# State-space layer of a four-layer backbone: u sent through DRAM by quarters, half of the contributions moved between the gate's chunks

## The chip, the cores and the metric

The kernel runs on one core of a Trainium2 chip. The metric is the device time of one execution in microseconds (us), as the median of repeated runs.

## The reference, cut to what matters

The backbone has four layers; layer 1 is the bidirectional diagonal state-space layer (S5) that this change is about. There are 384 tokens (128 of context, 256 latent), and 2048 channels in 128 groups of 16, each group with a complex state of 64.

```
u, gate = split(h @ w_in, 2)                 # 2048 + 2048 columns
for di in (forward, backward):
    bu[t] = b_bar @ u[t]                     # per group: 16 channels -> 64 complex states
    bu[edge] += a_bar * h0
    x[t] = a_bar * x[t -+ 1] + bu[t]         # the scan; context and latent tokens each on their own,
    yd[t] = real(c @ x[t])                   # latent tokens start from a given state
y = gelu(d * u + yd_forward + yd_backward)
y = y * sigmoid(y @ w_glu + b_glu)
out = (y * silu(gate)) @ w_out
```

## The kernel before, in words

Each core engine runs one program: TensorE (PE) the matmuls, ScalarE (ACT) and VectorE (DVE) the rest, GpSimd (POOL) and SyncE (SP) issue DMAs. Weights come in chunks of 1 MiB through a ring of four buffers. After each chunk of a layer's weight comes a chunk of `ada_w`, the modulation of the next layer, which PE takes with 4 matmuls from the ring (line 331). SP loads chunks in this one order (`load_chunk`, line 261): a chunk may be loaded when the chunk four places before it has been used, so an `ada_w` chunk waits for PE's matmuls on the one two chunks earlier, and everything behind it in SP's queue waits too. ACT rounds a chunk to `w_hi` (line 399, `split_chunk`), DVE makes the rest `w_lo` (line 406), and PE takes three products of it (`group_sums`, line 302, 48 matmuls for a chunk of u, gate or glu). Two `w_hi`/`w_lo` buffers alternate. Four chunks make a group of 512 output channels.

Layer 1 runs so:

- u: 4 groups. ACT and DVE copy the sums to `s5_uT` (lines 2350, 2444).
- When all of u is there, POOL stores it to DRAM (line 2199), waits, and gathers it back into `s5_u`, where rows are 8 tokens x 16 channels: two DMAs of single elements (line 2204) and eight of runs of 48 elements (line 2208). It runs beside the gate's chunks.
- gate: 4 groups; ACT writes SiLU of the sums to `s5_gateT`. Then all engines meet (`mix1.projected`), and POOL stores the gate to DRAM (line 2213).
- Contributions: for k of 0 to 15 (8 groups each), SP loads 1 MiB of prepared weights (`wk`, line 2230; `wk[0]` has a place of its own, `spare`; the other three lie over the hT tile's words in `scratch`), PE does 64 matmuls (line 2297), ACT and DVE copy them out of PSUM to the states `hs` (lines 463 and 2402).
- Scans: with 8 steps of tokens folded into the prepared weights, 31 steps remain; DVE scans states 0 to 7 of k (`hs[0]`), then 8 to 15 (`hs[1]`), with six instructions a step (lines 2425, 2431, 2435).
- Outputs: for each k, `cak` and `tk` are loaded (1 and 0.5 MiB, lines 2240, 2243), PE multiplies states by them (lines 2321, 2327), ACT copies (line 463), PE turns the result round (line 2338), ACT takes the gelu of it (line 2396). k = 0 waits for the contributions of all 16 k and the first scan, k = 8 for the second scan.
- y is split into hi and lo by quarters (lines 456, 460) after all 16 k, then glu's chunks begin.

Of the kernel before, what the change touches and what calls it, by code (L numbers as in the profile page):

```python
# [13 lines left out]
P = 128  # L14
# [116 lines left out]
def build(nc, ins, outs, consts, layers=range(DEPTH)):  # L131
    ctx = ExitStack()
    with ctx:
# [219 lines left out]
        def ada_rows(a):  # L353

            at = [place for end, place in ((8, 6144), (21, 22240), (24, 12800), (32, 12288), (36, 19200), (48, 12928)) if a < end]
            return view(at[0], GC)

        def act_ada(a):
            nc.scalar.wait_ge(ada_used, 4 * (a + 1))
            if a == ADA_START:  # L360
                nc.scalar.wait_ge(x_saved, 16)
            act_copy(ada_rows(a), banks[4][:, :])
            nc.scalar.drain().then_inc(ada_copied, 1)
# [1786 lines left out]
        spare = view(20224, 2048)  # L2150
        wk = [spare] + [hT_words[:, n * 2048:(n + 1) * 2048] for n in range(3)]
# [27 lines left out]
        bwd_taken_late = sem("bwd_taken_late")  # L2179
        scan_multiplied = sem("scan_multiplied")  # L2180
        scan_summed = sem("scan_summed")
        scan_stepped = sem("scan_stepped")
# [9 lines left out]
        def pool_s5(pool, l):  # L2192
            pool.wait_ge(h_lo_ready, h_quarter(f"norm{l}", 3))
            nc.gpsimd.dma_start(st_rows, w["state_s5"].rearrange("a b d (g h) n r -> (a b d g) (h n r)", h=2))\
                .then_inc(h0_in, 16)
            nc.gpsimd.memset(s5_u[:, :, SCH:SCE], 0.0).then_inc(u_zero, 1)

            pool.wait_ge(u_evacuated, 2)
            nc.gpsimd.dma_start(ud_dram.rearrange("(k p) n -> p k n", p=P), s5_uT).then_inc(u_parked, 16)
            pool.wait_ge(u_parked, 16)  # L2200
            pool.wait_ge(u_zero, 1)
            for rows, col, tok in ((slice(112, 128), SCH, 0), (slice(0, 16), SCH + 1, CTX - 1)):
                at = tok % ST * SCH + tok // ST
                nc.gpsimd.dma_start(s5_u[rows, :, col:col + 1],
                                    ud_dram[:, at:at + 1].rearrange("(g p) c -> p g c", p=SC),
                                    allow_slow_non_contiguous=True).then_inc(u_in, 16)
            for j in range(ST):
                nc.gpsimd.dma_start(s5_u[16 * j:16 * j + 16, :, 0:SCH],
                                    ud_dram[:, j * SCH:(j + 1) * SCH].rearrange("(g p) c -> p g c", p=SC))\
                    .then_inc(u_in, 16)  # L2210

            pool.wait_ge(stage_done, after(f"mix{l}.projected"))
            nc.gpsimd.dma_start(gate_dram, s5_gateT.rearrange("p a b -> p (a b)")).then_inc(gate_parked, 16)
            pool.wait_ge(y_ready, 8)
            nc.gpsimd.dma_start(s5_gate_back.rearrange("p a b -> p (a b)"), gate_dram).then_inc(gate_back, 16)
            pool.wait_ge(state_copied, 1)
            nc.gpsimd.dma_start(outs[4].rearrange("a b d (g h) n r -> (a b d g) (h n r)", h=2), st_rows)\
                .then_inc(state_stored, 16)
            pool.wait_ge(state_stored, 16)

        def sp_s5(sp, l):
            sp.wait_ge(x_saved, 16 * parked(l))
            for k in range(16):
                if k == 0:
                    sp.wait_ge(s5_w_stored, 16 * HB)
                if k == 1:
                    sp.wait_ge(stage_done, after(f"mix{l}.projected"))
                if k >= 4:
                    sp.wait_ge(s_ready, k - 3)
                nc.sync.dma_start(wk[k % 4], wbt_dram[k]).then_inc(wk_in[k % 4], 16)  # L2230
            for k in range(16):
# [4 lines left out]
                if k == 3:  # L2236
                    sp.wait_ge(s_ready, 13)
# [7 lines left out]
        u_evacuated = sem("u_evacuated")  # L2245

        def pe_s5(pe, st, l):
            for name in ("u", "gate"):
                for g in range(4):
                    first = (name, g) == ("u", 0)  # L2250
                    group_sums(pe, f"{name}{l}", g, [P] * 4, bank_wait=first_banks(l) if first else None,
                               inputs=f"norm{l}" if first else None)
# [3 lines left out]
            pe.wait_ge(h0_in, 16)  # L2256
            for r in range(2):
                nc.tensor.transpose(banks[7][:, r * P:(r + 1) * P], st_rows[:, r::2], ident[:, :])
            nc.tensor.drain().then_inc(h0_turned, 1)
            pe.wait_ge(u_in, 16 * (ST + 2))  # L2260

            for k in range(16):
                pe_contributions(pe, k)
# [11 lines left out]
            nc.tensor.drain().then_inc(state_turned, 1)  # L2275
            for g in range(4):
# [3 lines left out]

        def pe_contributions(pe, k):


            pe.wait_ge(wk_in[k % 4], 16 * (k // 4 + 1))
            if k >= 2:
                pe.wait_ge(fwd_taken, k - 1)
                if k < 10:
                    pe.wait_ge(bwd_taken, k - 1)
                else:
                    pe.wait_ge(bwd_taken_late, k - 9)  # L2290
            for gi in range(4):
                for d in range(2):
                    for r in range(2):
                        at = (2 * gi + r) * SCE
                        for h in range(2):
                            w0 = (2 * gi + h) * 256 + (2 * d + r) * SN
                            mm = nc.tensor.matmul(banks[2 * (k % 2) + d][64 * h:64 * h + 64, at:at + SCE],
                                                  wk[k % 4][:, w0:w0 + SN], s5_u[:, 8 * k + 2 * gi + h, :],
                                                  start=True, stop=True, skip_group_check=True)
            mm.then_inc(s_ready, 1)  # L2300

        def pe_outputs(pe, l, k):
# [4 lines left out]
            if k == 0:  # L2307
                pe.wait_ge(fwd_taken, 16)
                pe.wait_ge(bwd_taken_late, 8)
# [33 lines left out]
        def act_s5(act, st, l):  # L2343
            def u_write(g):
                for m in range(2):
# [3 lines left out]
                    bank_free(nc.scalar, m)  # L2349
            stream("act", f"u{l}", u_write)  # L2350
            nc.scalar.drain().then_inc(u_evacuated, 1)
# [6 lines left out]
            stream("act", f"gate{l}", gate_write)  # L2358
            st.at(f"mix{l}.projected")
            act.wait_ge(u_parked, 16)  # L2360
            for k in range(16):
                act.wait_ge(s_ready, k + 1)
                if k == 8:
                    act.wait_ge(gate_parked, 16)
                take_contributions(act_copy, k, 0).then_inc(fwd_taken, 1)
                if k >= 8:
                    take_contributions(act_copy, k, 1).then_inc(bwd_taken_late, 1)
            for k in range(16):
# [11 lines left out]
            split_h("act")  # L2380
# [18 lines left out]

        def take_contributions(copy, k, d):  # L2400
# [4 lines left out]
        def dve_scan(dve, half):  # L2405
# [3 lines left out]
            bk = banks[7][:, 0:2 * P].rearrange("p (r d h g) -> p r d h g", r=2, d=2, h=2)  # L2409
            for d, (zero, first) in enumerate(((0, 16), (15, 47))):  # L2410
                v.memset(h_[:, zero, d, :, :], 0.0)
                v.tensor_copy(h_[:, first, d, :, :], bk[:, :, d, half, :])
            v.drain()
            for s in range(31):
# [6 lines left out]
                for d in range(2):  # L2421
                    if s:
                        dve.wait_ge(scan_stepped, 2 * (31 * half + s - 1) + d + 1)
# [3 lines left out]
                                    .broadcast_to([P, 2, segs, 64]), ALU.mult).then_inc(scan_multiplied, 1)  # L2427
                for d in range(2):
                    dve.wait_ge(scan_multiplied, 2 * (31 * half + s) + d + 1)
                    t = [scan_t[:, d, w, 0:segs, :].rearrange("p s (r g) -> p s r g", r=2) for w in range(2)]  # L2430
                    v.tensor_tensor(t[0], t[0], t[1][:, :, ::-1, :], ALU.add).then_inc(scan_summed, 1)
                for d in range(2):
                    dve.wait_ge(scan_summed, 2 * (31 * half + s) + d + 1)
                    n_ = h_[:, nxt[d], d, :, :].rearrange("p s r g -> p s (r g)")
                    v.tensor_tensor(n_, n_, scan_t[:, d, 0, 0:segs, :], ALU.add).then_inc(scan_stepped, 1)
            v.drain().then_inc(scanned, 1)

        def dve_s5(dve, st, l):
            v = nc.vector

            def u_write(g):
                for m in range(2, 4):
# [3 lines left out]
                    bank_free(v, m)  # L2446
            stream("dve", f"u{l}", u_write)
            v.drain().then_inc(u_evacuated, 1)
            stream("dve", f"gate{l}")
            st.at(f"mix{l}.projected")  # L2450

            dve.wait_ge(u_parked, 16)
            for k in range(8):
                dve.wait_ge(s_ready, k + 1)
                take_contributions(v.tensor_copy, k, 1).then_inc(bwd_taken, 1)
            dve.wait_ge(h0_turned, 1)
            dve.wait_ge(fwd_taken, 8)
            dve.wait_ge(bwd_taken, 8)
            dve_scan(dve, 0)
            dve.wait_ge(fwd_taken, 16)  # L2460
            dve.wait_ge(bwd_taken_late, 8)
            dve_scan(dve, 1)
# [8 lines left out]
            split_h("dve")  # L2471
# [67 lines left out]
        def sp_program(sp):  # L2539
# [3 lines left out]
            for l in layers:  # L2543
# [12 lines left out]
                if l % 3 == 1:  # L2556
                    load_job(sp, f"u{l}", 4, w["s5_w_in"][j], 0)
                    load_job(sp, f"gate{l}", 4, w["s5_w_in"][j], D)
# [49 lines left out]
```

## Time and profile before

| what | value |
|---|---|
| median of 3 runs | 3464.74 us (3463.69 to 3467.09) |
| the profiled execution's own time | 3458.35 us |
| its span in the profile | 3456.6 us |
| PE busy | 3179.6 us (92%) |
| DVE busy, ACT busy | 1462.8 us (42%), 1062.3 us (31%) |
| chain that ended last, by engine | PE 67%, DVE 8%, DMA 7%, PEld 7% |
| mean granted clock of TensorE | 0.966 of full |

The span runs from the first to the last instruction. Busy time is the time in which an engine had an instruction under way. PEld is PE's loading of weights, which overlaps its matmuls. The chain that ended last is followed back from the last instruction, at each step to what released it. The granted clock is 1.0 at 2.4 GHz and 0.5 at 1.2 GHz.

### The profile page before, as it was taken

Reading aid. Unit: us, or ns where it says so; the run is one execution under the profiler, and the core shown is the slowest. Engines: PE = TensorE matmul, PEld = TensorE weight load, DVE = VectorE, ACT = ScalarE, POOL = GpSimd, SP = SyncE. Lnnn points to the kernel's source line nnn. Section 1 sums busy time; section 2 is a strip of 40 time slices with the busy share of each in tenths; the row PEclk is TensorE's granted clock in tenths of the full one; section 3 lists DMA queues with packets and bytes.
Section 4 is the critical chain, followed back from the end, with each engine's and each line's share of the span. In section 5 each row is a group of like instructions: output and inputs, shape, how many; then the busy total and the mean of one; then the engine's idle time right before and its main releaser. Section 6 shows DMA issues by size and latency. Waiting matters only on the chain.

```text
span 3456.6 us, 47210 instructions
## 1 busy us (share of the span) xinstructions
PE 3179.6 (92%) x20134; PEld 2659.4 (77%) x20134; DVE 1462.8 (42%) x2137; ACT 1062.3 (31%) x1433; POOL 185.5 (5%) x285
## 2 busy tenths in 40 slices
PE   5699899989899997879999899999999999999988
PEld 2488788866677986767988677886877998986777
DVE  3499852344434221192243454323334332244443
ACT  1333333222324212123232343323333323322322
POOL 1033330000000000000000000000000000000000
PEclk7899999999999998899999999999999999999999
DMA  9899985511364687785652555565443443421132
GB/s 357 312 334 353 316 295 210 199 57 37 110 214 165 219 219 196 271 321 216 219 192 79 178 200 190 183 215 195 163 167 118 132 125 121 136 88 37 37 124 96
DMA packets 288096, 639.18 MB, mean 185 GB/s; under 512 B 21280, under 2 KB 54192, under 8 KB 277264
## 3 DMA queue, kind: packets, MB, share of 16 engines
q1 hardware_dynamic: 262896, 524.58, 44.0%
q0 software_dynamic: 24992, 111.59, 9.4%
q8 instruction: 159, 2.61, 0.3%
q14 instruction: 49, 0.40, 0.0%
HBM read 561.01 MB, written 75.04 MB: 184 GB/s over the span
## 4 chain that ended last, share of the span: by engine, by line
PE 67%; DVE 8%; DMA 7%; PEld 7%; issue 4%; ACT 3%; PEldq 2%; DVEq 1%; ACTq 0%; POOL 0%; SPq 0%; POOLq 0%
PE bank L302 35%; PE bank L306 21%; PE bank L331 4%; DMA raw<-in_ada_w 3%; PEld bank L770 2%; DMA raw<-in_s_w_in 2%; PEld bank L764 2%; DVE arena L1996 1%; DVE w_lo L406 1%; DMA raw<-in_mla_w_in 1%; DVE arena L2425 1%; DMA s_in_dram<-arena 1%; PEld bank L820 1%; PE bank L609 1%; ACT hT_hi L456 1%
## 5 line engine op out<-in xcount | busy, mean ns | idle before, releaser
L406 DVE TENSOR_TENSOR w_lo<-raw,w_hi 128x2048 fp32r<-128x2048 f32 (+3 forms) x364 | 619.0, 1717 | 1216.3 <-ACTq L400 1212.5
L302 PE MATMUL bank<-hT_hi,w_hi 128*128 128x384 f32 (+1 forms) x2608 | 904.1, 347 | 56.9 <-DVEq L407 35.7
L399 ACT ACTIVATE w_hi<-raw 128x2048 fp32r<-128x2048 f32 (+3 forms) x364 | 521.5, 1452 | 1300.8 <-PE bank L302 670.6
L302 PE MATMUL bank<-hT_lo,w_hi 128*128 128x384 f32 (+1 forms) x2608 | 887.4, 340 | 0.0
L302 PE MATMUL bank<-hT_hi,w_lo 128*128 128x384 f32 (+1 forms) x2608 | 886.8, 340 | 0.0
L302 PEld LDWEIGHTS bank<-hT_hi,w_hi 128*128 128x128 f32 (+1 forms) x2608 | 493.7, 189 | 129.1 <-issue 82.2
L302 PEld LDWEIGHTS bank<-hT_lo,w_hi 128*128 128x128 f32 (+1 forms) x2608 | 493.9, 189 | 1.5
L302 PEld LDWEIGHTS bank<-hT_hi,w_lo 128*128 128x128 f32 (+1 forms) x2608 | 493.2, 189 | 1.4
L306 PE MATMUL bank<-w_hi,hT_hi 128*128 128x512 f32 x1056 | 424.7, 402 | 12.5 <-DVE hT_lo L460 12.2
L306 PE MATMUL bank<-w_lo,hT_hi 128*128 128x512 f32 x1056 | 419.5, 397 | 0.0
L306 PE MATMUL bank<-w_hi,hT_lo 128*128 128x512 f32 x1056 | 419.4, 397 | 0.0
L463 ACT ACTIVATE arena<-bank 128x512 f32<-128x512 f32 (+5 forms) x298 | 157.4, 543 | 383.2 <-PE bank L331 114.2
L306 PEld LDWEIGHTS bank<-w_hi,hT_hi 128*128 128x128 f32 x1056 | 200.9, 190 | 79.9 <-issue 35.2
L331 PE MATMUL bank<-raw,silu_pad 128*32 128x512 f32 x1536 | 213.9, 633 | 51.5 <-DMA raw<-in_ada_w 45.7
L306 PEld LDWEIGHTS bank<-w_hi,hT_lo 128*128 128x128 f32 x1056 | 200.7, 190 | 47.5
L306 PEld LDWEIGHTS bank<-w_lo,hT_hi 128*128 128x128 f32 x1056 | 200.9, 190 | 44.8
L1996 DVE TENSOR_TENSOR arena<-arena 128x896 f32<-128x896 f32 (+1 forms) x128 | 142.3, 1153 | 6.0 <-issue 4.5
L942 ACT ACTIVATE arena<-bank,small 128x384 f32<-128x384 f32 (+1 forms) x96 | 47.8, 507 | 255.1 <-DVEq L1104 255.1
L331 PEld LDWEIGHTS bank<-raw,silu_pad 128*32 128x32 f32 x1536 | 32.0, 110 | 113.7 <-DMA raw<-in_ada_w 66.4
L770 PE MATMUL bank<-w_hi,hT_hi 128*128 128x256 f32 x512 | 99.5, 288 | 5.5 <-DVEq L748 1.8
L764 PE MATMUL bank<-hT_hi,w_hi 128*128 128x512 f32 x256 | 85.3, 415 | 14.2 <-DVE hT_hi L1087 6.6
L770 PEld LDWEIGHTS bank<-w_hi,hT_hi 128*128 128x128 f32 x512 | 80.8, 188 | 18.6 <-issue 14.0
(324 smaller groups left out, 2739.8 us busy)
## 6 DMA issues: line engine op xcount, KB each, us to landing
raw<-in_ada_w SPq DMA_DIRECT2D x192, 1024.0 KB, 5.3
raw<-in_mla_w_in SPq DMA_DIRECT2D x64, 768.0 KB, 7.4
raw<-in_gla_w_in SPq DMA_DIRECT2D x48, 1024.0 KB, 7.5
raw<-in_mla_w_in SPq DMA_DIRECT2D x40, 1024.0 KB, 7.0
raw<-in_mla_w_out SPq DMA_DIRECT2D x32, 1024.0 KB, 5.3
raw<-in_s_w_in SPq DMA_DIRECT2D x32, 1024.0 KB, 7.5
s_out_dram<-arena POOLq DMA_DIRECT2D x32, 512.0 KB, 5.8
s_in_dram<-arena POOLq DMA_DIRECT2D x16, 1024.0 KB, 9.1
```

The costliest lines, as they stand in the source:

```text
L302: mm = nc.tensor.matmul(banks[m][0:width, 0:TOK], wp[:, slot, k, at:at + width], hp[:, kt, :], start=(first and n == 0), stop=(last and n ...
L306: mm = nc.tensor.matmul(banks[m][:, 0:cols], hp[:, kt, m * P:(m + 1) * P], wp[:, slot, k, 0:cols], start=(first and n == 0), stop=(last an ...
L331: mm = nc.tensor.matmul(banks[4][32 * k:32 * k + 32, :], silu_pad[:, at:at + 32], raw_of("ada", a, s)[:, k, :], start=(s == 0), stop=(s == ...
L399: nc.scalar.activation(dst, src_, ACT.Copy)
L406: nc.vector.tensor_tensor(dst, src_, pick(w_hi, *part)[0], ALU.subtract)
L456: nc.scalar.activation(hT_hi[:, k, :], h32[:, k, :], ACT.Copy)
L463: return nc.scalar.activation(out, in_, ACT.Copy)
L609: mm = nc.tensor.matmul(banks[6 + c][:, (k % 4) * P:(k % 4 + 1) * P], G_small[:, k, c:c + 1].broadcast_to([P, P]), ident[:, :], start=True ...
L764: mm = nc.tensor.matmul(banks[7][:, 0:KEYS], wp[:, slot, kt, j * 256:j * 256 + P], cp[:, kt, :], start=(kt == 0 and m == 0), stop=(kt == 3 ...
L770: mm = nc.tensor.matmul(banks[7][:, (t % 2) * 256:(t % 2 + 1) * 256], cp[:, kt, t * P:(t + 1) * P], wp[:, slot, kt, :].rearrange("p (h x) ...
L942: nc.scalar.activation(p_sb[:, h % 2, t, 0:b - a], score_bank(h, t), ACT.Exp, scale=SM_SCALE, bias=mx[:, t:t + 1], accum_out=sm[:, t:t + 1])
L1996: nc.vector.tensor_tensor(to, powers, f, ALU.mult)
```

## The change

In u's part, each group of u is stored to DRAM and gathered back into `s5_u` as soon as it is copied out, so there are four stores and 40 gathers in place of one and 10, of a quarter's size each. The gate is stored by quarters too.

The contributions of k = 0 to 7 move into the gate's groups: after gate chunk n (n of 1 to 8) PE does the 64 matmuls of k = n - 1, in two halves into banks 6 and 7; ACT takes half 0 and DVE half 1 two chunks later in their streams. SP loads `wbt_dram[k]` in two halves into `spare` for it, between the gate's chunks, after PE has read the halves before. DVE begins the first scan after gate chunk 11 of its stream: four steps after each of 6 chunks, the last 7 steps after `mix1.projected`. Only k = 8 to 15 are left after the gate. The wait of the first outputs is for these and the first scan. In the scan the three semaphores become one. y's hi and lo are split by quarters while the last outputs run: ACT after k = 13, 14, 15, DVE after each quarter's product with the gate; glu's first matmul waits for 15 of 16 gelus. `ada_w` chunks 28 to 31 are put down in another place.

```
@@ pool_s5
-            pool.wait_ge(u_evacuated, 2)
-            nc.gpsimd.dma_start(ud_dram.rearrange("(k p) n -> p k n", p=P), s5_uT).then_inc(u_parked, 16)
-            pool.wait_ge(u_parked, 16)
...
+            for q in range(4):
+                pool.wait_ge(u_written_act, q + 1)
+                pool.wait_ge(u_written_dve, q + 1)
+                part = ud_dram[q * GC:(q + 1) * GC, :]
+                nc.gpsimd.dma_start(part.rearrange("(k p) n -> p k n", p=P), s5_uT[:, 4 * q:4 * q + 4, :]).then_inc(u_parked, 16)
+                pool.wait_ge(u_parked, 16 * (q + 1))
+                groups = slice(32 * q, 32 * q + 32)
...
+                    nc.gpsimd.dma_start(s5_u[16 * j:16 * j + 16, groups, 0:SCH],
+                                        part[:, j * SCH:(j + 1) * SCH].rearrange("(g p) c -> p g c", p=SC))\
+                        .then_inc(u_in, 16)
@@ new, called after each gate chunk n is loaded
+        def sp_s5_ahead(sp, l, n):
...
+            if n == 0 or 3 <= n < 10:
+                k = max(n - 2, 0)
+                for half in range(2):
+                    if k:
+                        sp.wait_ge(half_ready[half], k)
+                    nc.sync.dma_start(spare[:, 1024 * half:1024 * half + 1024], wbt_dram[k][:, 1024 * half:1024 * half + 1024])\
+                        .then_inc(half_in[half], 16)
@@ pe_s5
+            for g in range(4):
+                group_sums(pe, f"gate{l}", g, [P] * 4, between=lambda s, g=g: pe_s5_states(pe, 4 * g + s))
...
-            for k in range(16):
+            for k in range(8, 16):
                 pe_contributions(pe, k)
...
+            pe.wait_ge(y_taken, 15)
@@ new
+        def pe_s5_states(pe, n):
...
+            if 1 <= n < 9:
+                k = n - 1
+                if k % 4 == 0:
+                    pe.wait_ge(u_in, 16 * (ST + 2) * (k // 4 + 1))
+                for half in range(2):
+                    pe.wait_ge(half_in[half], 16 * (k + 1))
+                    if k:
+                        pe.wait_ge(half_taken[half], k)
+                    elif half:
+                        pe.wait_ge(h0_turned, 2)
+                    for gi in (2 * half, 2 * half + 1):
+                        for d in range(2):
+                            mm = pe_contribution(spare, banks[6 + half], (4 * d + 2 * (gi % 2)) * SCE, k, gi, d)
+                    mm.then_inc(half_ready[half], 1)
@@ dve_s5
+                if 3 <= n < 11:
+                    take_half(dve, v.tensor_copy, 1, n - 3)
...
+                if n >= 11:
+                    dve_scan_steps(dve, 0, range(SCAN_AHEAD * (n - 11), SCAN_AHEAD * (n - 10)))
...
+                split_h("dve", [q])
@@ act_s5
+                if k >= 13:
+                    nc.scalar.drain()
+                    split_h("act", [k - 13])
```

## Rows read from the trace of the kernel before

**Rows 1.** Busy time of each engine, TensorE's granted clock and DMA in stages of layer 1.

```profile
core 0: us, PE busy (x) PEld busy (x) DVE busy (x) ACT busy (x) POOL busy (x), PEclk, DMA share, GB/s
1215.00:1252.00 37.00, 36.92 (x220) 32.73 (x219) 8.21 (x6) 7.32 (x6) 0.00 (x0) 1.00 0.61 214
...
1290.00:1330.00 40.00, 17.81 (x95) 15.98 (x96) 4.58 (x2) 7.68 (x8) 3.08 (x3) 0.70 1.05 155
...
1441.00:1478.00 37.00, 21.36 (x525) 20.48 (x526) 4.42 (x8) 4.19 (x9) 0.57 (x1) 0.72 0.98 389
```

**Rows 2.** SP's DMA issues from the last u chunk to the contributions, in time.

```profile
1251.39 0.37 SPq L261 DMA_DIRECT2D raw<-in_ada_w  x1
...
1271.99 0.51 SPq L261 DMA_DIRECT2D raw<-in_s_w_in  x1
...
1372.27 0.37 SPq L261 DMA_DIRECT2D raw<-in_ada_w  x1
...
1411.74 0.37 SPq L261 DMA_DIRECT2D raw<-in_ada_w  x1
...
1440.64 0.37 SPq L261 DMA_DIRECT2D raw<-in_ada_w  x1
...
1442.54 1.29 SPq L2230 DMA_DIRECT2D scratch<-s_in_dram  x3
```

**Rows 3.** The chain that ended last, 1260 to 1600 us, by pieces.

```profile
1271.99 36.82 DMA raw<-in_s_w_in
1308.84 1.91 ACT w_hi L399
1310.80 2.29 DVE w_lo L406
...
1361.63 8.65 PE bank L302 x48
...
1599.72 11.05 PE bank L302 x48
```

**Rows 4.** POOL's issues around u, in time.

```profile
1252.39 1.17 POOL L2199 DMA_DIRECT2D s_u_dram<-arena  x1 [149.64 <-ACTq L2351]
1270.45 2.07 POOL L2204 DMA_DIRECT2D arena<-s_u_dram  x2 [16.89 <-DMA s_u_dram<-arena]
...
1308.74 3.08 POOL L2208 DMA_DIRECT2D arena<-s_u_dram  x3 [31.10 <-issue]
```

**Rows 5.** DMA from 1270.5 to 1330 us: rate in 40 slices, queues, issues.

```profile
GB/s 380 77 132 285 280 65 115 96 101 121 128 103 108 141 117 102 111 141 101 104 130 104 99 102 202 383 384 390 384 133 111 93 125 123 92 97 133 99 96 99
...
q1 hardware_dynamic: 3040, 6.03, 52.8%
q0 software_dynamic: 986, 3.16, 52.0%
...
arena<-s_u_dram POOLq DMA_DIRECT2D x2, 8.0 KB, 8.5
```

**Rows 6.** Engines in order of time from 1453 to 1600 us.

```profile
1453.13 3.66 PE L2297 MATMUL bank<-arena 128*64 128x50 f32 x64 [9.94 <-DMA arena<-s_in_dram]
...
1468.09 2.03 PE L2297 MATMUL bank<-arena 128*64 128x50 f32 x64
...
1478.73 0.76 DVE L2425 TENSOR_TENSOR arena<-arena,a 128x256 f32<-128x256 f32 x2
...
1480.21 0.75 DVE L2425 TENSOR_TENSOR arena<-arena,a 128x256 f32<-128x256 f32 x2
...
1516.33 1.99 PE L2321 MATMUL bank<-scratch,arena 64*48 64x128 f32 x32 [14.74 <-DVEq L2436]
...
1554.62 1.17 PE L2321 MATMUL bank<-scratch,arena 64*48 64x128 f32 x32 [0.95 <-DVEq L2436]
...
1594.63 0.67 PE L2273 MATMUL bank<-ident,arena 128*32 128x128 f32 x16
...
1595.70 6.24 ACT L456 ACTIVATE hT_hi<-scratch 128x1536 fp32r<-128x1536 f32 x4
```

More of the change, by code:

```diff
@@ L353, in ada_rows @@
         def ada_rows(a):
-            at = [place for end, place in ((8, 6144), (21, 22240), (24, 12800), (32, 12288), (36, 19200), (48, 12928)) if a < end]
+            at = [place for end, place in ((8, 6144), (21, 22240), (24, 12800), (28, 12288), (32, 19712), (36, 19200), (48, 12928)) if a < end]
             return view(at[0], GC)
@@ L2207, in pool_s5 @@
[L2207 to L2213, printed above, removed]
+            for q in range(4):
[5 more added lines that the diff above has]
+                groups = slice(32 * q, 32 * q + 32)
+                for rows, col, tok in ((slice(112, 128), SCH, 0), (slice(0, 16), SCH + 1, CTX - 1)):
+                    at = tok % ST * SCH + tok // ST
+                    nc.gpsimd.dma_start(s5_u[rows, groups, col:col + 1],
+                                        part[:, at:at + 1].rearrange("(g p) c -> p g c", p=SC),
+                                        allow_slow_non_contiguous=True).then_inc(u_in, 16)
+                for j in range(ST):
+                    nc.gpsimd.dma_start(s5_u[16 * j:16 * j + 16, groups, 0:SCH],
+                                        part[:, j * SCH:(j + 1) * SCH].rearrange("(g p) c -> p g c", p=SC))\
+                        .then_inc(u_in, 16)
@@ L2214, in pool_s5 @@
+            for q in range(4):
+                pool.wait_ge(gate_written, q + 1)
+                nc.gpsimd.dma_start(gate_dram[:, 4 * TOK * q:4 * TOK * (q + 1)],
+                                    s5_gateT[:, 4 * q:4 * q + 4, :].rearrange("p a b -> p (a b)")).then_inc(gate_parked, 16)
             pool.wait_ge(y_ready, 8)
@@ L2236, in sp_s5 @@
                 if k == 3:
[L2237 removed]
+                    sp.wait_ge(s_ready, 5)
                 if k >= 4:
@@ L2243, in sp_s5 @@
                 nc.sync.dma_start(tk(l, k % 3), k_dram[k].rearrange("j p g n -> (j p) g n")).then_inc(tk_in[k % 3], 16)
-        u_evacuated = sem("u_evacuated")
-        def pe_s5(pe, st, l):
[L2248 to L2252, printed above, removed]
+        u_written_act = sem("u_written_act")
+        u_written_dve = sem("u_written_dve")
+        gate_written = sem("gate_written")
+        half_in = [sem(f"half_in{n}") for n in range(2)]
+        half_ready = [sem(f"half_ready{n}") for n in range(2)]
+        half_taken = [sem("half_taken_act"), sem("half_taken_dve")]
+        def pe_s5(pe, st, l):
+            for g in range(4):
+                group_sums(pe, f"u{l}", g, [P] * 4, bank_wait=first_banks(l) if g == 0 else None,
+                           inputs=f"norm{l}" if g == 0 else None)
+            for g in range(4):
+                group_sums(pe, f"gate{l}", g, [P] * 4, between=lambda s, g=g: pe_s5_states(pe, 4 * g + s))
             pe_ada_turn(pe, 31)
             st.at(f"mix{l}.projected")
[L2256 to L2262, printed above, removed]
+            for k in range(8, 16):
                 pe_contributions(pe, k)
@@ L2279, in pe_s5 @@
                 pe_ada_turn(pe, ADA_LAYER * (l + 2) - 1)
-        def pe_contributions(pe, k):
[L2284 to L2290, printed above, removed]
+        def pe_s5_states(pe, n):
+            if n == 0:
+                pe.wait_ge(h0_in, 16)
+                for r in range(2):
+                    mm = nc.tensor.transpose(banks[7][:, r * P:(r + 1) * P], st_rows[:, r::2], ident[:, :])
+                mm.then_inc(h0_turned, 1)
+            if 1 <= n < 9:
+                k = n - 1
+                if k % 4 == 0:
+                    pe.wait_ge(u_in, 16 * (ST + 2) * (k // 4 + 1))
+                for half in range(2):
+                    pe.wait_ge(half_in[half], 16 * (k + 1))
[7 more added lines that the diff above has]
+                    mm.then_inc(half_ready[half], 1)
@@ new lines, in pe_contribution @@
+        def pe_contribution(weights, bank, at, k, gi, d):
+            for r in range(2):
+                for h in range(2):
+                    w0 = (2 * gi + h) * 256 + (2 * d + r) * SN
+                    mm = nc.tensor.matmul(bank[64 * h:64 * h + 64, at + r * SCE:at + (r + 1) * SCE],
+                                          weights[:, w0:w0 + SN], s5_u[:, 8 * k + 2 * gi + h, :],
+                                          start=True, stop=True, skip_group_check=True)
+            return mm
@@ L2291, in pe_contributions @@
+        def pe_contributions(pe, k):
+            pe.wait_ge(wk_in[k % 4], 16 * (k // 4 - 1))
+            if k >= 10:
+                pe.wait_ge(fwd_taken, k - 9)
+                pe.wait_ge(bwd_taken, k - 9)
+            elif k == 8:
+                pe.wait_ge(u_in, 16 * (ST + 2) * 4)
             for gi in range(4):
                 for d in range(2):
[L2293 to L2299, printed above, removed]
+                    mm = pe_contribution(wk[k % 4], banks[2 * (k % 2) + d], 2 * gi * SCE, k, gi, d)
@@ L2357, in gate_write, with states @@
                     bank_free(nc.scalar, m)
-            stream("act", f"gate{l}", gate_write)
-            st.at(f"mix{l}.projected")
[L2360 to L2364, printed above, removed]
+                nc.scalar.drain().then_inc(gate_written, 1)
+            def states(g, s):
+                n = 4 * g + s
+                if 3 <= n < 11:
+                    take_half(act, act_copy, 0, n - 3)
+            stream("act", f"gate{l}", gate_write, states)
+            st.at(f"mix{l}.projected")
+            act.wait_ge(gate_parked, 16 * 4)
+            for k in range(8, 16):
+                act.wait_ge(s_ready, k - 7)
                 take_contributions(act_copy, k, 0).then_inc(fwd_taken, 1)
-                if k >= 8:
-                    take_contributions(act_copy, k, 1).then_inc(bwd_taken_late, 1)
+                take_contributions(act_copy, k, 1).then_inc(bwd_taken, 1)
             for k in range(16):
@@ L2398, in act_take_outputs, with take_half @@
                 .then_inc(y_taken, 1)
+        def take_half(eng, copy, half, k):
+            eng.wait_ge(half_ready[half], k + 1)
+            if k == 0:
+                eng.wait_ge(u_parked, 16 * 4)
+            for d in range(2):
+                cp = copy(hs[0][:, 1 - d:50 - d, d, :, 4 * k + 2 * half:4 * k + 2 * half + 2].rearrange("p c r g -> p r c g"),
+                          banks[6 + half][:, d * 4 * SCE:(d + 1) * 4 * SCE]
+                          .rearrange("p (g r c) -> p r c g", g=2, r=2)[:, :, d:49 + d, :])
+            cp.then_inc(half_taken[half], 1)
         def take_contributions(copy, k, d):
@@ L2403, in take_contributions, with dve_scan_start, dve_scan_steps @@
                         banks[2 * (k % 2) + d][:, 0:8 * SCE].rearrange("p (g r c) -> p r c g", g=4, r=2)[:, :, d:49 + d, :])
-        def dve_scan(dve, half):
+        def dve_scan_start(half):
             v = nc.vector
             h_ = hs[half]
-            bk = banks[7][:, 0:2 * P].rearrange("p (r d h g) -> p r d h g", r=2, d=2, h=2)
+            first_states = st_rows.rearrange("p (r d h g) -> p r d h g", r=2, d=2, h=2)
             for d, (zero, first) in enumerate(((0, 16), (15, 47))):
                 v.memset(h_[:, zero, d, :, :], 0.0)
-                v.tensor_copy(h_[:, first, d, :, :], bk[:, :, d, half, :])
+                v.tensor_copy(h_[:, first, d, :, :], first_states[:, :, d, half, :])
             v.drain()
-            for s in range(31):
+        def dve_scan_steps(dve, half, steps):
+            v = nc.vector
+            h_ = hs[half]
+            for s in steps:
                 segs = 2 if s < 15 else 1
@@ L2422, in dve_scan @@
                     if s:
-                        dve.wait_ge(scan_stepped, 2 * (31 * half + s - 1) + d + 1)
+                        dve.wait_ge(scan_moved, 6 * (31 * half + s - 1) + 4 + d + 1)
                     c_ = h_[:, cur[d], d, :, :].rearrange("p s r g -> p s (r g)")
@@ L2557, in sp_program @@
                     load_job(sp, f"u{l}", 4, w["s5_w_in"][j], 0)
-                    load_job(sp, f"gate{l}", 4, w["s5_w_in"][j], D)
+                    for n in range(16):
+                        load_parts(sp, f"gate{l}", w["s5_w_in"][j], D, GC, n, n + 1)
+                        sp_s5_ahead(sp, l, n)
                     load_parts(sp, f"glu{l}", w["s5_w_glu"][j], 0, GC, 0, 2)
```

79 lines of the change are left out of this document (40 added, 39 removed).

## Prediction, made before the changed kernel ran

> **What bounds the kernel now.** I read the page first: PE is busy 92% of the span and carries two thirds of the chain that ended last, so time is gained only where PE waits, and lost wherever PE gets more to do. Then I read the stages of layer 1 [rows 1]. In u's part PE is busy 36.92 of 37 us, with DMA at a share of 0.61 and 214 GB/s: PE sets the time there. In 1290 to 1330 us PE is busy 17.81 of 40, the DMA engines are full (1.05) and yet move only 155 GB/s: this is the gathering of u. In 1441 to 1478, the contributions, PE has 21.36 of 37 and DMA is full at 389 GB/s: loads bound. Of the scans the reader sees one wait of 14.74 us of PE's first outputs on DVE, and 0.95 us at the second scan [rows 6]. I then laid out the order of events on SP's and POOL's queues [rows 2, 4], and the chain, to see which wait carries the end [rows 3].
>
> **How large the holes are.** The gate's part runs from the issue at 1251.39 (PE is through u's last chunk) to that at 1440.64 (through the gate's last): 189.25 us for four groups. A group without disturbance is 1411.74 - 1372.27 = 39.47 us [rows 2], four are 157.9. So the gathering costs 31.4 us, low clock included (0.70 of full in that stretch). The chain shows how: the load issued at 1271.99 lands 36.82 us later, and only then ACT and DVE split it [rows 3]. From 1270.5 to 1330 the loads got 6.03 MB and POOL's queue 3.16 MB, most of the time at about 110 GB/s; only in slices 26 to 29 (of 1.49 us), from about 1306 to 1313, the rate is 384: POOL had run dry (its next issue comes after 31.10 us, at 1308.74) [rows 4, 5].
>
> I set t = 0 at 1442.5, where the engines have met after the gate. Before, the first outputs start at t = 73.8 (1516.33) and the second half of them at t = 112.1 (1554.62) [rows 6].
>
> **u by quarters.** The bytes and runs are the same, cut in four. Slow gathering took 1272.5 to 1306 and 1313 to 1330, 50.5 us [rows 4, 5], so a quarter's is 12.6 us, preceded by a store of 0.75 MiB, which I take as 6 us (the whole took 1270.45 - 1252.39 = 18 us). Loads get about half of the 110 GB/s in it. Between bursts of 39.5 us distance the engines have 0.39 of their time free [rows 1], some 15 us, so the burst fits on average. What decides is whether one load comes too late. A load issued after a chunk is used two chunks on, 19.3 us or more later (two of 9.64 us, which is 39.47 less 0.9 for turning the rows of `ada_w`, by four); landed, it needs 1308.84 to 1313.1, 4.3 us, for its splits [rows 3]. It may thus land 15.0 to 15.5 us after its issue. The pair of loads issued as the store begins has about 1.35 of 2 MiB in when the gather starts 5.5 us later; the other 0.7 at 60 GB/s needs 11 to 12, so it lands 16 to 17 us after its issue: 1 to 2 us late. The next pair gets 4 us of the slow rate, then 390 GB/s, and lands 15 us after issue, just in time. I take 1.25 us a quarter, 5 us in all. The bounds are 0 and, if the loss goes by the time spent gathering wherever it lies, the whole 31.4. Gain 26.4 us (0 to 31.4).
>
> **Contributions of k = 0 to 7 on PE between gate chunks.** They are moved out of a stage that waits for DMA into one where PE is full, so they count in full: 64 matmuls take 2.03 us at a clock of 1.0 (3.66 at 0.5) [rows 6], and I add 0.1 us for the two waits and the change of weights: 8 x 2.13 = 17.0 us. Their loads, 8 MiB, now share the gate's DMA: a slot is then 9.64 + 2.13 = 11.8 us and needs 3 MiB, 8.1 us at 389 GB/s, so it fits. On SP the halves wait for PE's reading of the halves before, right after the `ada_w` part that SP has just waited for; behind them in SP's queue stands the next gate chunk, which so is issued 2.1 us later and lies behind 1 MiB (2.7 us). 3 MiB at 389 GB/s are 8.1 us, with 2 us to begin and land some 10, of the 17 that it now may take: no stall. Should each slot's wait for weights show, I bound it at 3 us, 24 us in all.
>
> ACT gets two copies a slot (0.3 us each, an estimate from the 392 elements in 0.5 of one now), DVE the same: both wait for PE most of the time (DVE is busy 8 of 37 us [rows 1]), so nothing. The scan steps: a step of two segments is 1480.21 - 1478.73 = 1.48 us [rows 6], four are 5.9. DVE's split ends 4.3 us after a chunk's end, so it is done with the steps at 10.3, and the next `w_hi` is there at 9.64 + 1.91 = 11.6: covered. Were it not, the split would have 5 us more before PE needs it.
>
> **After the gate.** Before, k = 0 had its weights asked for at the last and shared DMA with the gate's 3 MiB store; PE waited 9.94 us for them [rows 6]. Now k = 8 has its weights. The gate's store has 0.75 MiB left. To be loaded before the first outputs: the last `ada_w` MiB, 7 of weights, 0.75 of store, 1.5 of the outputs' own, 10.25 MiB or 27.6 us at 389 GB/s from 1441.5; that is t = 26.6. I take t = 27. The last contributions are in PSUM at t = 24.7 and taken at 25.7 (22 to 30). The first scan is over by then: its last seven steps take about 7 us. The second runs from 25.7 for 1516.33 - 1478.73 = 37.6 us, to t = 63.7 with its start-up. PE's first eight outputs took 1516.33 to 1553.67 (1554.62 - 0.95), 37.3 us, so they end at t = 64.3, and nothing waits for the scan. I take t = 64.4 for k = 8, against 112.1: gain 47.7 us. The bounds: the loads land 4 us earlier or 6 later, gain 42 to 52. The outputs' own pace stays (1.5 MiB each need 4.0 us, a k takes 37.3 / 8 = 4.7).
>
> **y by quarters.** Before, PE is through with its small matmuls at 1595.3, glu starts at 1599.72, and its first chunk takes 11.05 in place of 8.65 us, at a fallen clock [rows 3, 6]. 4.4 + 2.4 = 6.8 us. Now three quarters are split before, and PE waits for the 15th gelu only (about 1594.7). The last outputs get 1.56 us more of ACT at k = 13, 14 and 15 (6.24 / 4 [rows 6]). PE waits for ACT's copies and gelus there, of two k earlier, so most of it is hidden by a k's 4.7 us; uncovered it would be 4.7 us. I give back 0.7: gain 6.1 us (2 to 7).
>
> **Sum.** -47.7 + 17.0 - 26.4 - 6.1 = -63.2 us. One semaphore in place of three, `ada_w`'s other place and the split scan set-up cost nothing on PE's path. From the profiled execution's 3458.35 this gives 3395.2 us. The median of the runs shown lies 6.4 us higher, at 3464.74, so the forecast for it is 3401.5. A difference of 0.2%, 7 us, is what a measurement tells from no change.
>
> **What the skill says against it.** In 1270.5 to 1330 the two DMAs of 8 KB landed in 8.5 us [rows 5], and POOL's issue of the first two took 2.07 us [rows 4]. The Trainium skill, DMA: Bandwidth & Descriptors, Bandwidth, says that transfers under 64 KB are bound by their descriptors and that DMAs should be batched to 1 MiB or more. The gathers go from 384 to 96 KB. Its section on the fixed cost gives about 2 us for each DMA, mostly completion; 30 more DMAs would be an estimated 60 us of it, which if it held the engines would be 15 a quarter on top of 12.6. The trace before has no gather of that size to decide this.
>
> **Rivals.**
> 1. *Each burst starves the loads as before*, 7.8 us a quarter: for it speaks that my pair lands within 2 us of its limit; against it that the first load to come late was issued after the gathering began (1271.99 against 1270.45), and would have been due at 1287, when a quarter's 12.6 us are over [rows 2, 4]. Then -47.7 + 17.0 + 0 - 6.1 = -36.8: 3428. Chance 0.2.
> 2. *The gate's slots wait for their weights*, or the next gate chunk is late behind them, 3 us each: 24 us more, 3425. Against it the sum of 3 MiB in 11.8 us; for it that SP's single queue puts PE's contributions ahead of the ring's refilling. Chance 0.12.
> 3. *A gather costs by the DMA, not by its bytes*: a quarter's ten DMAs take as long as the ten did, so a quarter starves the ring by 31.4 us, 125.6 in all. -47.7 + 17.0 + 94.2 - 6.1 = +57.4, 3522, slower. It decides from 23 us lost a quarter on (62.9 + 31.4 = 94.3, by four, is 23.6). Against it: the eight went at a steady rate by bytes, and the 8 KB ones landed sooner [rows 5]. The skill's rule of the paragraph above points this way, to a part of it. Chance 0.04.
> 4. *The stage after the gate doesn't shrink as far*: the outputs starve for `cak` or `tk`, or the second scan becomes the wait, as DVE and PE end within 1 us of each other. 10 us more: 3412. Chance 0.14.
>
> The forecast itself has 0.5: its own range is 3391 to 3412. The range for 8 in 10 reaches to rivals 1 and 2: 3386 to 3430. Faster by over 0.2% in all but rival 3 and the unforeseen: 0.94; within 0.2% 0.02; slower 0.04.
>
> **What the profile after would show.** Right: in u's part bursts of DMA share 1.0 after each group with hardly a wait of PE on DVE's split; a gate's part of about 157.9 + 17 + 5 = 180 us; after it PE's contributions at once, first outputs 27 us after the engines meet, no wait on the scan over 1 us; glu starting within 1 us of the state matmuls at the full clock. Wrong: waits of PE on `w_lo` 10 to 20 us after each u group (rival 1), or at each of the slots 1 to 8 before the contributions (rival 2).

## The result, and the profile after

The changed kernel takes 3415.0 us (median of 4 runs, 3405.88 to 3419.57), the kernel before 3464.22 beside it: ratio 0.985, 95% interval 0.9836 to 0.9864. Run again twice it gave 0.9844 (0.982 to 0.9868; 3411.97 us) and 0.9837 (0.9816 to 0.9859; 3406.91 us). So the change brings 52 to 57 us by these ratios (49, 53 and 59 by the medians) where 63 were forecast. 3415.0 lies in the range of 3386 to 3430, and 3 us above the forecast's own 3391 to 3412; the two repetitions lie in that.

To follow this through the profile, layer 1 is cut in four stretches: u and gate (from SP's issue of the first `ada_w` chunk in u's part to the end of PE's turning of the last one), from there to the first outputs, the 16 outputs, and on to glu's first matmul.

| us | before | after | change | forecast |
|---|---|---|---|---|
| u and gate | 338.9 | 329.0 | -9.9 | -9.4 |
| to the first outputs | 74.0 | 29.4 | -44.6 | -46.9 |
| 16 outputs | 78.4 | 86.4 | +8.0 | -0.8 |
| to glu | 5.0 | 1.0 | -4.0 (and -2.4 in glu's first chunk) | -6.1 |

The sum is -52.9. The span fell by 45.0 only (3456.6 to 3411.6): the changed kernel's profiled execution came to u's first issue 6.0 us later (1109.50 against 1103.50), in a stretch that the change doesn't touch, and lost 1.9 us behind glu's first chunk.

The chain that ended last, from u's groups to the outputs, answers to [rows 3]:

```profile
1149.90 16.06 DMA raw<-in_s_w_in
...
1191.09 16.39 DMA raw<-in_s_w_in
...
1232.62 14.54 DMA raw<-in_s_w_in
...
1281.78 2.03 PE bank L2327 x64
1283.83 11.57 DMA arena<-s_in_dram
...
1318.79 2.00 PE bank L2327 x64
...
1438.67 8.93 DMA scratch<-s_in_dram
```

Read here, first, that the load under way at each of the first three bursts of gathering now lands 14.5 to 16.4 us after its issue, not 36.8 (17.35 us at the fourth, which lies beside the gate's first chunks and is not on the chain). Second, a slot's 64 contribution matmuls are 2.0 us, and no wait for weights lies before them but one of 0.8 us at the second slot. There is the slow rate too: the second half of the weights of k = 1, issued in the burst after u's last group, is 11.57 us under way. PE's waits for the split of the weights in u and gate are 4.1 us:

```profile
PE bank L302 <- DVEq L407: 4.1, 3, 2.0
```

(columns: us in total, times, longest). After the gate, the stretches; they answer to [rows 1]:

```profile
1438.70:1467.90 29.20, 19.11 (x516) 18.41 (x517) 7.25 (x47) 7.08 (x16) 0.00 (x0) 0.82 0.99 392
1467.90:1505.00 37.10, 31.28 (x770) 25.94 (x770) 37.10 (x186) 11.30 (x21) 0.00 (x0) 1.00 0.95 374
```

DMA is full until the first outputs, at 392 GB/s, as it was in the sum. But it is nearly full (0.95) in the first 37 us of the outputs as well, where [rows 6] began with their weights at hand. PE in order of time there:

```profile
1485.46 0.84 PE L2382 MATMUL bank<-ident,mrow 48*64 48x48 f32 x22 [0.23 <-issue]
...
1486.20 1.11 PE L2365 MATMUL bank<-scratch,arena 64*48 64x128 f32 x30
1487.24 0.64 PE L2371 MATMUL bank<-mrow,arena 128*48 128x128 f32 x8
1487.81 1.17 PE L2365 MATMUL bank<-scratch,arena 64*48 64x128 f32 x32
1488.91 0.64 PE L2371 MATMUL bank<-mrow,arena 128*48 128x128 f32 x8
1489.48 0.89 PE L2382 MATMUL bank<-ident,mrow 48*64 48x48 f32 x22
1491.95 0.49 PE L2382 MATMUL bank<-ident,mrow 48*64 48x48 f32 x9 [1.57 <-issue]
```

PE stops for 1.57 us in the middle of a run of 32 like matmuls (line 2382), for nothing that the profile shows. No wait of the program stands there. Between the two stops lie 22+5+30+8+32+8+22 = 127 matmuls (the 5 are those left out at "..."); the next two stretches, up to stops of 0.92 and 2.52 us, have 125 and 127. Each matmul has a weight load, so that is some 254 instructions. The page's queue "q8 instruction" moved 2.61 MB in 159 packets, 16.4 KB each, 65 bytes for each of 254. So the theory: PE gets its instructions by DMA, in pieces of 16 KB, and when the DMA engines are full a piece comes late. The waits that the profile puts down to nothing ("issue") add up to 11.0 us in the changed kernel's outputs, against 5.3 in those before, and in the 88 us around these outputs that queue brings 15 packets:

```profile
PE bank L2365 <- issue: 6.0, 4, 2.5
PE bank L2382 <- issue: 4.1, 4, 2.1
PE bank L2371 <- issue: 0.9, 1, 0.9
...
q8 instruction: 15, 0.25, 1.0%
```

The traces also have the time of each packet, and it decides between chance and cause. Of the nine stops of this profile, eight end 1.3 to 1.6 us after the end of a 16 KB packet of that queue. In the outputs of all 13 profiles 82 of 88 stops do so (1.2 to 1.6 us); if packets and stops had nothing to do with each other, fewer than one in ten would. The other six are short, 0.2 to 0.5 us. So PE goes on when a packet of instructions has come.

### The profile page after: what moved, and what is told of

It reads as the page before. It is cut to its first block, busy times and chain, and to the rows that moved or that the text cites. A ratio compares the mean times of both kernels' runs of the same rounds, so it can differ in the third digit from the quotient of the medians.

```text
span 3411.6 us, 47297 instructions
## 1 busy us (share of the span) xinstructions
PE 3181.1 (93%) x20134; PEld 2659.9 (78%) x20134; DVE 1464.5 (43%) x2146; ACT 1063.3 (31%) x1441; POOL 203.7 (6%) x321
## 3 DMA queue, kind: packets, MB, share of 16 engines
q8 instruction: 159, 2.61, 0.3%
## 4 chain that ended last, share of the span: by engine, by line
PE 70%; PEld 7%; DMA 7%; DVE 5%; issue 4%; ACT 3%; PEldq 2%; DVEq 1%; ACTq 0%; POOL 0%; SPq 0%; POOLq 0%
PE bank L302 35%; PE bank L306 21%; PE bank L331 5%; DMA raw<-in_ada_w 3%; PEld bank L770 3%; PEld bank L764 2%; DMA raw<-in_s_w_in 1%; DVE w_lo L406 1%; PE bank L2365 1%; DVE arena L1996 1%; DMA raw<-in_mla_w_in 1%; PEld bank L820 1%; PE bank L346 1%; PE bank L609 1%; ACT hT_hi L456 1%
```

## The experiments

**u by quarters alone.** In the kernel before, the store and the gathers by quarters as in the change, nothing else:

```
-            nc.gpsimd.dma_start(ud_dram.rearrange("(k p) n -> p k n", p=P), s5_uT).then_inc(u_parked, 16)
+            for q in range(4):
+                pool.wait_ge(u_written_act, q + 1)
+                pool.wait_ge(u_written_dve, q + 1)
...
-            pe.wait_ge(u_in, 16 * (ST + 2))
+            pe.wait_ge(u_in, 16 * (ST + 2) * 4)
```

> The kernel before, with u alone sent through DRAM by quarters; contributions, scan and y as before. Theory (short bursts of slow gathering end before the ring of loads runs dry): the part from u's first ada issue to the gate's last, 337.1 us before, falls by 31.4 less 5, to about 311, with three or four waits of PE of 1 to 3 us after u's groups; the whole is 26 us faster (ratio 0.9925). Rival (the loss goes by the time spent gathering): 337, no change. Rival (a gather costs by the DMA): over 400.

Ratio 0.9956 (0.9938 to 0.9973), -15 us; u and gate took 315.4 us in the profiled execution (-23.5), which was the second fastest of ten (3438 to 3465 us; the profiled 3439.5). So the quarters gain nearly what they were to in good executions, but only 15 us of the 26 expected over all ten (18 by the medians). Executions spread more than before. Neither "no change" nor "over 400 us" holds.

**By halves.** The same with two bursts (`range(2)`, each after two groups).

> The same by halves, two bursts of about 25 us each. Theory (a burst costs only what it outlasts the ring's 15 us of slack by): each burst costs some 9 us, so the part takes about 324, halfway between; 13 us faster than before. If the loss went by the time spent gathering, one, two and four bursts would cost the same 31 us; if only the number of bursts mattered, the loss would be half of 31 from two and a quarter from four.

Ratio 0.9995 (0.9983 to 1.0007): on the whole time 2 us, not told from no change, where 13 were expected. In the profiled execution u and gate took 331.7 us, 7.2 less than with one burst. The chain:

```profile
1197.92 26.59 DMA raw<-in_s_w_in
...
1281.74 22.07 DMA raw<-in_s_w_in
```

In one profiled execution each, one burst costs 31.4 us, two cost 24.2, four 7.9 (in the second fastest of ten; by the ratio and the medians of all ten, four cost 13 to 16). The same bytes and runs, so the loss doesn't go by the time spent gathering. Nor does it halve with the burst, or two would have cost 16. From the first gather's issue to the last one's landing, the two bursts were 31 and 27 us long, not 25, and a quarter's are 17 to 18. The two let the load under way land 26.6 and 22.1 us after its issue, far over the 15 that it may take; with the four, alone in the kernel before, it landed after 14.0 to 17.6. The order is as expected; of the 13 us expected, 7 are found in the stretch and 2 in the whole.

**y by quarters alone**, in the kernel before:

```
-            split_h("act")
+                if k >= 13:
+                    nc.scalar.drain()
+                    split_h("act", [k - 13])
...
+            pe.wait_ge(y_taken, 15)
```

> The kernel before, with y alone split into hi and lo by quarters and glu waiting for 15 gelus. Theory: PE's wait before glu of 4.4 us falls under 1 and glu's first chunk takes 8.7 in place of 11.05 us; 6 us faster (ratio 0.998). Rival (the splits on ACT delay the last outputs by as much): 0 to 2 us.

Ratio 0.9985 (0.9975 to 0.9996), -5 us. The interval alone, 1 to 9 us, doesn't put the rival out; the profile does: glu starts 0.99 us after PE's last turned output, not 5.02, its first chunk takes 8.66 us, not 11.05, and the outputs are no longer (82.7 us) than in the two kernels above, which split y as before (82.3 and 82.0).

**The outputs without their loads.**

```
-                nc.sync.dma_start(cak[k % 4], ca_dram[k]).then_inc(cak_in[k % 4], 16)
+                if k < 4:
+                    nc.sync.dma_start(cak[k % 4], ca_dram[k]).then_inc(cak_in[k % 4], 16)
...
-            pe.wait_ge(cak_in[k % 4], 16 * (k // 4 + 1))
+            pe.wait_ge(cak_in[k % 4], 16)
```

> The changed kernel, with the loads of the outputs' weights (cak, tk) left out from k = 4 and 3 on, so that these k use the first ones' weights; PE's instructions are the same. In the changed kernel the 16 outputs take 86.4 us, with idle times of PE of 0.2 to 2.5 us at about every 128th matmul, in the middle of runs. Theory (PE's own instructions come by DMA, 16 KB at a time, and come late when the 16 DMA engines are full of loads): the idle times all but vanish outside of the 3 MiB read of the gate, and the outputs take about 70 us. Rival (the gaps are PE's own, whatever DMA does): they stay, 84 us or more. Rival (the loads themselves are late): the time falls too, but the gaps in the changed kernel would stand at the first matmul of a k, not in the middle.

This kernel leaves out loads and so computes other outputs; it ran once. Its 16 outputs took 75.2 us, at a DMA share of 0.27, with PE's waits:

```profile
PE bank L2367 <- DVEq L2537: 3.3, 1, 3.3
...
PE bank L2367 <- issue: 0.2, 1, 0.2
```

The stops fell from 11.0 to 0.2 us, with the same instructions, and the packets of instructions came here too. So the stops hang on the loads beside them, and by their spacing and the packets' times they are waits for PE's own instructions. How long they get isn't told by DMA's share alone: with the gathers paced (below) the first eight outputs had a share of 0.97 and 2.5 us of stops, in the changed kernel 0.87 and 6.4. The outputs took 75 and not 70, since PE now runs into the second scan (3.3 us, then at a fallen clock, the next 32 matmuls taking 1.99 in place of 1.17 us): without the stops, DVE is the bound of the first half, as rival 4 had it.

**The first scan after the gate**, in the changed kernel:

```
-                if n >= 11:
-                    dve_scan_steps(dve, 0, range(SCAN_AHEAD * (n - 11), SCAN_AHEAD * (n - 10)))
...
-            dve_scan_steps(dve, 0, range(SCAN_AHEAD * 6, 31))
+            dve_scan_steps(dve, 0, range(31))
```

> The changed kernel, with the first scan's steps all after the gate (none between its chunks). Theory: the first scan then ends 38 us after the engines meet in place of 7, the first outputs start at 38 and not at 29, and the second scan follows it from 38 to 76, so that the second half of the outputs waits for it until 76 instead of starting at 71: 5 to 9 us slower than the changed kernel. Rival (the load of weights hides the scan anyway): no difference.

Ratio to before 0.9847 (0.9822 to 0.9872); the changed kernel on the same chip 0.9844. The first outputs waited, as expected, but the time did not grow:

```profile
PE bank L2365 <- DVEq L2528: 10.2, 1, 10.2
```

First outputs at 37.8 us in place of 30.4, and the outputs then took 81.1 in place of 86.5: 118.9 against 116.9 us. What the scan's early start gives to PE, the loads take back: during a wait of PE they run ahead, and the outputs stop less (5.5 us, in place of 9.9 in the changed kernel on that chip). The expectation, 5 to 9 us, rested on the scan as the bound and missed; its rival was right.

**The changed kernel again**, beside that and the next two, and once more in the last group.

> The changed kernel once more, on the chip of the three beside it, to compare them with it and to see how its stages spread from one execution to the next. Ratio to the kernel before 0.985 (0.983 to 0.988). The part of u and the gate takes 329 us (337 before), the outputs 82 to 88 us.

> The changed kernel beside the two below. Ratio to the kernel before 0.984 to 0.985.

Its u and gate took 331.3 and 336.9 us, where the first profile has 329.0; its outputs 86.5 and 82.1. In the execution of 336.9 us PE waits for the split 2.75 us at 1207.0 and 3.3 us at 1252.5, and with both the granted clock falls to 0.5 for some microseconds, in u's part:

```profile
1185.00:1225.00 40.00, 37.25 (x200) 33.91 (x201) 10.29 (x6) 9.24 (x7) 5.98 (x10) 0.91 0.79 209
1225.00:1265.00 40.00, 36.65 (x210) 32.41 (x209) 7.99 (x5) 7.79 (x7) 7.04 (x11) 0.96 0.89 246
```

In the first profile of the changed kernel, with waits of at most 2.0 us, it is 1.00 there. The chunk after the load that landed 17.21 us after its issue takes 11.38 in place of 8.72 us, the one after the second wait 10.23. With 7.7 us of waits for the split, 1.0 for a slot's weights and these 4.2 us, 12.9 of the 13.4 us over the undisturbed time are found.

**Gathers paced by the chunks**, in the changed kernel:

```
                 for j in range(ST):
+                    if j in (2, 4, 6):
+                        pool.wait_ge(lo_ready, chunk(f"u{l}", q, 3) + 3 + j // 2)
                     nc.gpsimd.dma_start(s5_u[16 * j:16 * j + 16, groups, 0:SCH],
```

> The changed kernel, with the eight gathers of a quarter sent off two at a time, the second, third and fourth pair each only after one more chunk of the weights has been split. Theory (a burst of slow gathering costs what it outlasts the ring's slack by): the waits of PE on the split after u's groups, 5.5 us of the 329 in the profiled execution and more in others, vanish; the part takes 324 us and executions spread less; 5 to 15 us faster than the changed kernel. Rival (time spent gathering counts wherever it lies): no change.

3408.02 us (3404.0 to 3410.15), ratio to before 0.983 (0.9808 to 0.9851), with 3411.97 for the changed kernel in the same group. The intervals overlap, so of the 5 to 15 us expected the whole shows no certain gain (4 us by the medians); the stretch does. u and gate took 323.7 us, and PE's wait for the split is

```profile
PE bank L302 <- DVEq L407: 0.4, 1, 0.4
```

Undisturbed, the stretch would take 338.9 - 31.4 = 307.5 us, with eight slots of 2.0 us 323.5. That is what is measured, with all the gathering in it: the same bytes and DMAs, spread, cost nothing. The rival, that time spent gathering counts wherever it lies, is out.

**Weights earlier.**

```
-                    sp.wait_ge(stage_done, after(f"mix{l}.projected"))
+                    sp.wait_ge(sums_ready, SUMS[f"gate{l}", 3] + 4)
```

> The changed kernel, with the loads of the weights of k = 9 to 11 issued as soon as PE has finished the gate's last sums, not after the engines have met (2.5 to 3 us later). Theory (27 us of loads set the start of the first outputs, at the full rate of DMA): the first outputs start 2.5 us sooner after the last sums; 2 to 3 us faster than the changed kernel. Rival (PE or the scan sets the start): no change.

Ratio 0.9837 (0.9808 to 0.9866): not told from the changed kernel. SP could not go as early as thought: ahead of this load in its queue stands an `ada_w` load that waits for PE's matmuls on the chunk before, so the loads were issued 1.5 us sooner against PE's last turning, not 2.5; the first outputs came at 29.5 us, in place of 29.4 to 30.4. The theory wasn't put to the test as it was meant.

**The gate read back by quarters**, after k = 7, 9, 11, 13:

```
-            pool.wait_ge(y_ready, 8)
+            for q in range(4):
+                pool.wait_ge(y_ready, 8 + 2 * q)
```

> The changed kernel, with the 3 MiB read of the gate during the outputs cut into four, after k = 7, 9, 11 and 13. Theory (PE's instructions come late when DMA is full): the same bytes in shorter bursts leave fewer fetches late in the second half of the outputs (idle for no shown reason of 2.2 and 2.1 us in it): 0 to 3 us faster than the changed kernel. Rival (bytes alone count): no change.

Ratio 0.9827 (0.9812 to 0.9842), the changed kernel in the same group 0.9837 (0.9816 to 0.9859). The stops in the outputs are 6.2 us in its profiled execution and 9.4 in the changed kernel's there; the times can't be told apart.

**All three together.**

> The changed kernel with the paced gathers, the earlier weights and the gate read by quarters together. Theory: the paced gathers' 5 us and about 1 us from each of the others: part of u and the gate 324 us, 5 to 9 us faster than the changed kernel, ratio to the kernel before 0.982 to 0.983.

3404.95 us (3397.77 to 3407.41), ratio 0.9824 (0.9808 to 0.984). It is the lowest of the medians of kernels that compute the layer in full, 2 us below the changed kernel beside it (3406.91), within the uncertainty; u and gate again took 323.9 us.

## Why the prediction was right, and where it was off

- **u by quarters: the mechanism was right, the term too small.** Forecast 26.4 us gained, 5 left. The seven profiled executions with the changed kernel's gathers (the change three times, scan after the gate, weights earlier, gate read by quarters, outputs without loads) took 329.0, 331.3, 336.9, 334.2, 332.8, 333.8 and 329.6, 332.5 in the mean, 9.0 over the undisturbed 323.5. The step that failed: "I take 1.25 us a quarter", where 2.3 were found. Three of its parts were off. A quarter's store took 9 to 11 us, not 6, and its gathers 17 to 18 us, not 12.6. The load that came late was not the pair issued with the store (in the first profile it landed within 11.3 us) but the next one, issued within 2 us of the first gather, for which the prediction had "just in time". And lateness was priced as waiting alone, while the clock fell with seven of the ten longest waits. Halves and paced gathers show that a burst's length against the ring's slack is the cause. Rival 1, each burst starving the loads as before (7.8 us a quarter), is out for the changed kernel by these profiles; the first run of quarters alone, with 13 to 16 us left over its ten executions, came near halfway to it.
- **Contributions between the chunks: right.** 17.0 forecast, 8 x 2.0 = 16 found, and the profiles show 1.1 us at most of waits for weights in all the slots together. Rival 2 is out.
- **After the gate: right, a little small.** First outputs 29.4 to 30.4 us after the meeting, forecast 27. The bytes were as summed, at 392 GB/s, but the sum lets them flow from 1 us before the engines meet. In the profile the last `ada_w` load is asked for 1.7 us before that, and DMA, idle until then, brings under 100 GB/s for 2 us. PE's wait of 6.7 us for k = 9 costs nothing by itself, since the loads behind it set the first outputs.
- **The outputs: the step "the outputs' own pace stays" failed.** It took 37.3 us for the first eight and 78.4 for all from the one profile. The pace hangs on DMA: the kernels with u by quarters, by halves and y's split alone, whose outputs are those of before, took 82.3, 82.0 and 82.7 us. The changed kernel took 82.1 to 86.5. That this is since its outputs start with no weights at hand is likely, by the scan after the gate (81.1 us, started 7 us later), but not shown: with the gathers paced they start so too and took 80.2. The load of 1.5 MiB in 4.0 us was weighed against PE's 4.7, and that PE's instructions go the same way was not seen. It costs about 3 us on the kernels' typical times, 8 in the two profiles compared: 5.7 of these are stops, and PE's busy time is 2.7 longer, at a clock of 0.90 in the second half, where it was 1.00.
- **The scan**: it is no longer what sets the outputs, but its early start by itself is worth 2 us, within the uncertainty, not the 5 to 9 expected. The 45 us gained there come from moving half of the contributions, with their 8 MiB of loads and 3/4 of the gate's store, out of a stretch that loads bound. Before, the path was 36 us of loads until the first scan could start, then its 38 us; with the scan after the gate it starts at once and still takes 38, and in the changed kernel 29 us of loads are left. Which part is the bytes and which the scan's inputs being there, no run separates.
- **y by quarters: right.** 6.1 forecast; 5 in the whole, 6.4 in the two profiles.

Together: 4 of the gathers, 2.5 to the first outputs and 3 in the outputs, less 1 of the contributions, are 8.5 of the 9 us by which -63 missed the -54 of the three comparisons. That is near the size of rival 4 (the stage after the gate shrinks 10 us less) for the two last terms, by stops that it didn't name; the second scan became a wait of over 1 us only without the loads. The whole still came out in the range by its width: the forecast's own range held it twice of three times.

Rival 3, a gather costing by the DMA, is out. The Trainium skill, DMA: Bandwidth & Descriptors, Bandwidth, says to batch DMAs to 1 MiB or more. Here a quarter's ten DMAs, the large ones of 96 KB, landed within 17 to 18 us of the first one's issue, 69 us for the four against 61 for the ten before, and with the gathers paced the 30 more DMAs cost nothing that can be seen, some 7 us of POOL's time to issue each quarter aside.

## What to carry to other kernels

A transfer of short runs beside a stream of loads cost nothing here when it was spread, 2 us a burst when a burst was just over the slack of the ring of buffers (17 us against 15), and 12 to 31 us a burst, about half its length, when it was twice or four times that; so cut it, and tie the pieces to the consumer's progress; moving work from a stretch that DMA bounds to one that PE bounds gives back the work's loads, minus PE's plain time for it; what is left in the emptied stretch is bound by bytes, so ask there what else uses DMA before starting anything earlier. When PE stops in the middle of like matmuls, count the instructions between the stops, and look at what the instruction queue's packets do.

## What the runs showed of the hardware

- In 1270.5 to 1330 us of the kernel before, loads and gathers had 52.8% and 52.0% of the DMA engines' time, and the loads moved 6.03 MB in it, 101 GB/s, where they alone draw 389 when asked for. That each queue gets its turn whatever it brings agrees with the Trainium skill, DMA: Bandwidth & Descriptors, Queues, rings and completion order: engines go round the queues packet by packet.
- Beside a stream of loads (DMA share 0.7 to 0.97) PE stops at multiples of about 127 matmuls, 0.2 to 3.2 us at a time, and goes on 1.2 to 1.6 us after a 16 KB packet of the queue "q8 instruction" has ended (82 of 88 stops); 5.3 to 11.0 us in 16 outputs, 0.2 without their loads, at a share of 0.27.
- In u's part and the gate's first chunks, in the eight profiles with four unpaced bursts, waits of PE of at most 2.1 us left the granted clock at 1.00, 2.4 GHz. Of ten waits of 2.5 to 3.4 us, seven had 3.4 or 6.8 us at 0.5, 1.2 GHz, with them, and three had none (2.6, 2.8 and 3.3 us). So the length of the wait alone doesn't tell it.
